# Attention bias in an encoder layer on Trainium2: from flip products on TensorE to a skewed copy in DRAM and additions on VectorE

## What is computed

```python
bias = rel_table[rel_bucket(kpos[None, :] - qpos[:, None])]
bias = jnp.transpose(bias, (2, 0, 1)).astype(jnp.float32)
visible = (kpos[None, :] // CHUNK) <= (qpos[:, None] // CHUNK)
s = jnp.einsum('bqhmd,bkhmd->bhmqk', qblk, k).astype(jnp.float32)
s = s + bias[None, :, None]
s = jnp.where(visible, s, -jnp.inf)
p = jax.nn.softmax(s, axis=-1)
attn = p[:, :, 0] - lam * p[:, :, 1]
```

## Time and profile before

| | |
|---|---|
| median of 3 runs | 537.84 us (536.12 to 542.68) |
| the profiled execution | 541.47 us, of which 539.7 us is the span of the profile |
| PE busy | 511.6 us, 95% of the span |
| DVE busy | 246.5 us, 46% |
| ACT busy | 196.8 us, 36% |
| DMA | 149.29 MB, mean 277 GB/s |
| chain that ended last | issue 46%, PE 40%, DVE 8%, DMA 3% |

### The profile page before, as it was taken

The page is one execution under the profiler, slowest core; times in us unless marked ns, Lnnn a source line. Parts: engine busy times, 40 slices in busy tenths (PEclk is TensorE's granted clock), DMA queues, the critical chain, the costliest instruction groups (busy, mean ns, idle before and its releaser), DMA issues.

```text
span 539.7 us, 7303 instructions
## 1 busy us (share of the span) xinstructions
PE 511.6 (95%) x2868; PEld 345.8 (64%) x2868; DVE 246.5 (46%) x466; ACT 196.8 (36%) x347; POOL 15.6 (3%) x30
## 2 busy tenths in 40 slices
PE   8799999899999999999989988999999999999782
PEld 7798998688888888898978533433443344333231
DVE  4473499967778679975652611111111111111113
ACT  6353567464736355354565202110211021101013
POOL 2000010000040000000000000000000000000000
PEclk9989999999999999999998899999999999999997
DMA  7777547633655548976997599999999999999982
GB/s 245 238 268 205 161 122 233 199 90 117 175 177 164 167 149 249 364 257 184 367 346 264 187 335 389 387 387 386 387 386 386 387 386 387 387 386 388 385 303 82
DMA packets 81835, 149.29 MB, mean 277 GB/s; under 512 B 8262, under 2 KB 11524, under 8 KB 81796
## 3 DMA queue, kind: packets, MB, share of 16 engines
q1 hardware_dynamic: 81780, 148.76, 80.2%
q10 hardware_dynamic: 16, 0.00, 0.0%
HBM read 147.69 MB, written 1.05 MB: 276 GB/s over the span
## 4 chain that ended last, share of the span: by engine, by line
issue 46%; PE 40%; DVE 8%; DMA 3%; ACT 2%; SPq 0%; POOLq 0%; POOL 0%; ACTq 0%; DVEq 0%
PE bank L1349 11%; PE bank L1351 11%; PE bank L1350 11%; DMA raw<-in_w_in 3%; DVE wl L877 3%; PE bank L1372 1%; PE bank L1468 1%; DVE xc L893 1%; ACT wh L539 1%; PE bank L1491 1%; PE bank L1465 1%; DVE big L923 1%; DVE al L863 1%; DVE big L1171 1%; DVE small L1160 0%
## 5 line engine op out<-in xcount | busy, mean ns | idle before, releaser
L877 DVE TENSOR_TENSOR wl<-raw,wh 128x1024 fp32r<-128x1024 f32 (+1 forms) x80 | 94.2, 1195 | 45.9 <-ACT wh L539 44.5
L539 ACT ACTIVATE wh<-raw 128x1024 fp32r<-128x1024 f32 (+1 forms) x80 | 82.2, 1042 | 79.2 <-PE bank L1351 60.5
L1349 PE MATMUL bank<-wh,ah 128*128 128x512 f32 (+2 forms) x248 | 93.8, 378 | 0.0
L1351 PE MATMUL bank<-wh,al 128*128 128x512 f32 (+2 forms) x248 | 92.8, 374 | 0.0
L1350 PE MATMUL bank<-wl,ah 128*128 128x512 f32 (+2 forms) x248 | 92.7, 374 | 0.0
L1276 DVE TENSOR_TENSOR kT<-bank,normg 64x512 f32<-64x512 f32 x16 | 11.0, 688 | 130.3 <-ACT normg L771 130.3
L1349 PE MATMUL bank<-ah,wh 128*128 128x256 f32 x176 | 51.2, 291 | 3.5 <-DVE wl L877 2.9
L1351 PEld LDWEIGHTS bank<-wh,al 128*128 128x128 f32 x248 | 46.7, 188 | 8.6
L1349 PEld LDWEIGHTS bank<-wh,ah 128*128 128x128 f32 x248 | 46.7, 188 | 8.1
L1350 PEld LDWEIGHTS bank<-wl,ah 128*128 128x128 f32 x248 | 46.7, 188 | 7.9
L1351 PE MATMUL bank<-ah,wl 128*128 128x256 f32 x176 | 50.5, 287 | 0.0
(11 more groups left out here) (330 smaller groups left out, 833.7 us busy)
## 6 DMA issues: line engine op xcount, KB each, us to landing
raw<-in_w_in SPq DMA_DIRECT2D x48, 512.0 KB, 4.4
gates<-in_w_exp_gate SPq DMA_DIRECT2D x15, 512.0 KB, 10.7
gates<-in_w_exp_up SPq DMA_DIRECT2D x15, 512.0 KB, 11.4
wh_raw<-in_w_exp_gate SPq DMA_DIRECT2D x15, 512.0 KB, 10.5
wl_raw<-in_w_exp_up SPq DMA_DIRECT2D x15, 512.0 KB, 11.5
raw<-in_w_branch SPq DMA_DIRECT2D x12, 512.0 KB, 3.9
conv_raw<-in_w_exp_up SPq DMA_DIRECT2D x10, 512.0 KB, 11.5
raw<-in_w_exp_gate SPq DMA_DIRECT2D x10, 512.0 KB, 10.8
```

Of the source, the lines that this page charges most:

```text
L539: act.activation(dst, src, ACT.Copy, scale=scale).then_inc(done, 1)
L877: dve.tensor_tensor(wl[:, n % RING, 0:sz], raw[:, n % RING, 0:sz], wh[:, n % RING, 0:sz].bitcast(F32), ALU.subtract)\
L1349: pe.matmul(dst, st[0], mv[0], start=start, stop=False, skip_group_check=True)
L1351: return pe.matmul(dst, st[1], mv[0], start=False, stop=stop, skip_group_check=True)
```

## The change

- `scratch` in DRAM becomes [4, 128, 384]. One DMA writes each head's run 128 times, from the same four partitions of `pr`.
- `toep` becomes [128, 4, 384] and is read with a step of 383 elements between partitions, starting at element 127 of the first copy: each query's row then stands in its own partition, unflipped, 256 columns for block t = 1 and 128 for t = 0. That takes two DMAs for each head instead of one.
- GpSimd masks both blocks, on partitions 0 to 63; it no longer builds `flip`.
- PE makes the four score products of a head alone; the four flip products go.
- VectorE adds the bias while it moves the scores from PSUM to `pr` in SBUF, one addition of 128 x 384 for each m, and takes the maxima from there, two reductions for both m instead of four. ScalarE's exponentials work in place in `pr`.
- The score banks are given back to PE after the additions (`score_biased`) instead of after the exponentials.
- `vec` (parameters that PE transposes early) moves into `pr`, columns 512 to 639.

```diff
-        toep = sb("toep", [P, HEADS, S])
+        toep = sb("toep", [P, HEADS, S + P])
-        vec = sb("vec", [50, P])
+        vec = pr[0:50, 512:512 + P]
-        scratch = nc.dram_tensor("bias_runs", [HEADS, 384], F32, kind="Internal").ap()
+        scratch = nc.dram_tensor("bias_runs", [HEADS, P, 384], F32, kind="Internal").ap()
...
-                    sp.dma_start(scratch, run[:, 0:384]).then_inc(s_("run_out"), 16)
+                    sp.dma_start(scratch, run[:, 0:384].unsqueeze(1).to_broadcast([HEADS, P, 384])).then_inc(s_("run_out"), 16)
...
                     for h in range(HEADS):
-                        sp.dma_start(toep[:, h, :], bass.AP(scratch.tensor, 384 * h, [[1, P], [1, S]]))\
-                            .then_inc(s_("toep_in"), 16)
+                        for at, lo, w in ((0, 0, S), (S, P, P)):
+                            sp.dma_start(toep[:, h, at:at + w], bass.AP(scratch.tensor, 384 * P * h + P - 1 + lo, [[383, P], [1, w]]))\
+                                .then_inc(s_("toep_in"), 16)
...
-            link(g.memset(flip[:, :], 0.0))
-            link(g.affine_select(out=flip[:, :], in_=flip[:, :], compare_op=ALU.not_equal, fill=1.0, base=-(P - 1),
-                                 pattern=[[1, P]], channel_multiplier=1))
...
-            g.wait_ge(s_("toep_in"), 16 * HEADS)
-            g.memset(toep[64:P, :, S - SEEN:S], LOW).then_inc(s_("toep_ready"), 1)
+            g.wait_ge(s_("toep_in"), 16 * 2 * HEADS)
+            for hi in (S, S + P):
+                g.memset(toep[0:64, :, hi - SEEN:hi], LOW).then_inc(s_("toep_ready"), 1)
...
-                for m, src in enumerate((pS1, pS0)):
+                for m in range(2):
                     for j, (lo, hi) in enumerate(((0, 256), (256, 384))):
-                        act.activation(pr[:, 384 * m + lo:384 * m + hi], src[:, lo:hi], ACT.Exp, bias=mx[:, 2 * m + j:2 * m + j + 1],
+                        p_ = pr[:, 384 * m + lo:384 * m + hi]
+                        act.activation(p_, p_, ACT.Exp, bias=mx[:, 2 * m + j:2 * m + j + 1],
...
             def score_max(h):
+                if h == 0:
+                    dve.wait_ge(s_("toep_ready"), 2)
                 dve.wait_ge(s_("scores_pe"), h + 1)
                 for m, src in enumerate((pS1, pS0)):
-                    for j, (lo, hi) in enumerate(((0, 256), (256, 384))):
-                        ins = dve.tensor_reduce(mx[:, 2 * m + j:2 * m + j + 1], src[:, lo:hi], AX.X, ALU.max)
+                    dve.tensor_tensor(pr[:, 384 * m:384 * m + 384], src[:, 0:384], toep[:, h, :], ALU.add).then_inc(s_("score_biased"), 1)
+                dve.wait_ge(s_("score_biased"), 2 * h + 2)
+                for j, (lo, hi) in enumerate(((0, 256), (256, 384))):
+                    ins = dve.tensor_reduce(mx.rearrange("p (m j) -> p m j", j=2)[:, :, j],
+                                            pr[:, :].rearrange("p (m n) -> p m n", m=2)[:, :, lo:hi], AX.X, ALU.max)
...
                 if h:
-                    pe.wait_ge(s_("score_exp"), 4 * h)
+                    pe.wait_ge(s_("score_biased"), 2 * h)
...
-                    pe.matmul(d, qT[QK * m:QK * m + QK, h, P * t:P * t + P], kT[QK * m:QK * m + QK, h, 0:w],
-                              start=(t == 1), stop=False, skip_group_check=True)
-                for t, w, lo, _, d in blocks:
-                    mm = pe.matmul(d, flip[:, :], toep[:, h, lo:lo + w], start=False, stop=True, skip_group_check=True)
+                        mm = pe.matmul(dst[:, 256 * (1 - t):256 * (1 - t) + w], qT[QK * m:QK * m + QK, h, P * t:P * t + P],
+                                       kT[QK * m:QK * m + QK, h, 0:w], start=(t == 1), stop=True, skip_group_check=True)
```

More of the change, by code:

```diff
@@ L175, in program @@
         ident = sb("ident", [P, P])
-        flip = sb("flip", [P, P])
         upper = sb("upper", [P, P])
         ones = sb("ones", [P, P])
-        vec = sb("vec", [50, P])
+        vec = pr[0:50, 512:512 + P]
         vecT = sb("vecT", [P, 50])
@@ L1460, in scores @@
                 if h:
-                    pe.wait_ge(s_("score_exp"), 4 * h)
-                blocks = [(t, w, lo, m, dst[:, 256 * (1 - t):256 * (1 - t) + w])
-                          for t, w, lo in ((1, 256, 0), (0, 128, 128)) for m, dst in enumerate((pS1, pS0))]
-                for t, w, _, m, d in blocks:
-                    pe.matmul(d, qT[QK * m:QK * m + QK, h, P * t:P * t + P], kT[QK * m:QK * m + QK, h, 0:w],
-                              start=(t == 1), stop=False, skip_group_check=True)
-                for t, w, lo, _, d in blocks:
-                    mm = pe.matmul(d, flip[:, :], toep[:, h, lo:lo + w], start=False, stop=True, skip_group_check=True)
+                    pe.wait_ge(s_("score_biased"), 2 * h)
+                for t, w in ((1, 256), (0, 128)):
+                    for m, dst in enumerate((pS1, pS0)):
+                        mm = pe.matmul(dst[:, 256 * (1 - t):256 * (1 - t) + w], qT[QK * m:QK * m + QK, h, P * t:P * t + P],
+                                       kT[QK * m:QK * m + QK, h, 0:w], start=(t == 1), stop=True, skip_group_check=True)
                 mm.then_inc(s_("scores_pe"), 1)
@@ L1530, in _ @@
                             mm.then_inc(s_("pool_pe"), 1)
-                    pe.wait_ge(s_("toep_ready"), 1)
                     for nm in ("q", "k"):
@@ L1543, in _ @@
                 if s == 4:
-                    pe.wait_ge(s_("score_exp"), 4 * HEADS)
+                    pe.wait_ge(s_("score_biased"), 2 * HEADS)
                     pe.wait_ge(s_("silu_done"), 3)
```

## The result

| | before | with the change |
|---|---|---|
| median | 539.1 us (4 runs, 536.12 to 542.68) | 570.76 us (4 runs, 568.53 to 573.02) |
| ratio | 1 | 1.0574, 95% interval 1.0527 to 1.0620 |
| profiled execution, span | 541.47, 539.7 us | 573.02, 571.3 us |

What follows compares the result with a forecast made beforehand. PE's progress before about 310 us was taken to bound the kernel. Stall 24.1, clock 1.7 and attention 2.3 made 28.1 us, giving 569.6 us for the profiled execution and 566 as the median; range 541 to 573.

Steps and rivals of the forecast that it cites:

- What bounds it: Before about 310 us PE's progress sets the weight stream's start, so a microsecond lost there arrives at the end undiminished.
- The write of the runs: Around 28 us: 786 KB in 512 rows from four partitions share one path of 25.4 GB/s, taking 31 us; chance 0.64.
- T: The duration of the write of the runs, taken as 31 us.
- B: Rival on the write: four engines work side by side, 10 us, total 545 us; chance 0.19.
- C: Rival on the write: spread wider or source cached, under 6.9 us and hidden, total 540 us; chance 0.10.
- 4/128 of the full rate: Full-rate loads spread over 128 partitions, so four neighbouring partitions were never seen to pass more than 13 GB/s.
- four completion marks: Four packets under 512 bytes at 29.0 to 30.0 us, read as showing that the small write used four of 16 engines.
- The stall: PE waits for chunk 8, whose load queues behind the write: T - 6.9 us, 24.1 us with T = 31.
- The clock: After PE's long idle time the granted clock falls to 0.72 over 6 us: 1.7 us lost.
- The flip products go, VectorE's chain grows: Attention slots: PE saves 5.4 us, VectorE gains 1.05 us a head, so the stage ends 2.3 us later.
- my replay: Slot-by-slot timing of the four heads, with PE idle 1.7, 2.5, 0.9 and 2.5 us ahead of their transposes.
- At nothing: Four more reads of `toep` (2 us at most if their cover went), masks, earlier bank release and moved `vec` cost nothing.

Runs made afterwards that it cites:

- bias moved behind the scores: The changed kernel with runs built in and written from 128 partitions, plus the gate block's bias addition and tanh moved behind the score work: 544.55 us, ratio 1.0063.
- woven order: The changed kernel with runs written from 128 partitions, other VectorE work between maxima and mixing, ScalarE's copies ahead of the exponentials: 538.96 us, ratio 0.9959.
- the variant at full clock: The changed kernel with the small write of before, `toep` read with a step of 1, bias rows in reversed order: 541.82 us, ratio 1.0013.
- the wide variant: The changed kernel, but VectorE builds the runs in all 128 partitions and the write reads each partition's own copy: 543.71 us, ratio 1.0046.

## Why the prediction was right, and where it was off

**What bounds it.** Right. A loss on PE before 310 us arrives at the end: the added time is 33.4 us at the logits' products and 31.6 at the end, and the 1.9 between them is the stretch of 13 or 15 us, which I take for chance.

**The write of the runs.** The step that decides. T was taken as 31 us and came out as 32.5, since the path carried 24.2 GB/s where I had put one engine's 25.4; rivals B (10 us) and C (under 6.9) are each seen in a variant with another source (8.5 us, 3.1 us), so they were true of other writes and not of this one. The argument of 4/128 of the full rate was loose (only an absence of evidence), and the variants put it on firm ground. The "four completion marks" were read rightly (the large write has four as well), but they say only how many engines, not how many paths.

**The stall.** 24.1 us forecast, 26.7 measured. The formula chunk 8 = 29.5 + T + 1.3 + 2.3 was off in two terms: the first packet came at 31.1 and not 29.5, 1.4 us behind an issue that itself started 1 us later and took 0.78 us instead of 0.28, and T was 1.5 us longer. The term of 1.3 us held: the last completion mark of chunk 8 (64.89 us) comes 1.28 us behind that of the write (63.61), and ScalarE starts 0.35 us later. With 0.3 us there and 0.2 in copy and subtraction, that is 3.6 us late, less the 1.0 by which PE itself came later. That the issue of chunk 8's load would take 9.3 us, and that nothing of the loads would flow until 40 us, was not foreseen; it did no harm, because the parts on the write's four engines come last anyway.

**The clock.** 1.7 us forecast, 2.5 measured at chunk 8, because PE ran at the low level past 72 us here, where the row I took it from the earlier trace rows averages 0.72 over 6 us. A second fall at slot 0, 1.0 us, was not foreseen. It is no plain sequel of the stall: it is there in the changed kernel and in the variants with partitions 0 to 3 and 0, 4, 8, 12, but also in two variants with no stall (bias moved behind the scores; woven order), and not in the two with idle products. PE waits 1.9 us ahead of slot 0 in every trace, and the clock falls behind it in some. What decides that is open.

**The flip products go, VectorE's chain grows.** 2.3 us forecast for the stage, 2.2 measured, 2.2 in the variant at full clock. Per head 1.05 us forecast and 1.06 measured, but that close by luck, as two errors cancel: additions and reductions take 2.05 us and not 2.20 (no wait of 0.15 for its own additions shows), and the wait for ScalarE's exponentials, now in place from SBUF, is 1.93 us and not 1.78, which I had counted as the same. Where PE waits was half wrong: I had all of it ahead of the transposes (1.7, 2.5, 0.9, 2.5); at full clock it is 1.45 there for head 0, then 1.27 + 0.66, 0.08 + 0.28, and 1.76 + 0.28, of which the first parts stand ahead of `attn_o`. They add up to 5.8 us and not to the 7.6 of my replay, and the stage is as long all the same, because, by the same estimate, a wait costs more than the idle time shown. ScalarE's copies for `attn_o` lie behind the exponentials in its order, so the same lateness of VectorE reaches PE first by that way.

**At nothing.** The eight reads of `toep` and the masks: between chunk 8 and slot 0 the trace shows no loss beside the clock's (2.5 us against 2.6 by the clock's levels), and none at all in the wide variant (63.5 us), which reads `toep` in the same eight transfers.

**The sum.** 28.1 forecast, 31.6 measured on the profiled executions. Of the difference of 3.5, 2.7 is the stall, 0.8 + 1.0 the clock, 1.0 the late start, -0.1 the stage and -1.9 the stretch before the experts. The two that I take for chance, 1.0 and -1.9, come to -0.9, towards the forecast. The rest up to 570.76 is that before had a median of 539.1 over four runs, 1.3 above the one I set out from.

## What to carry to other kernels

Before a broadcast in DRAM is built from a few rows in SBUF, count the groups of four partitions that the source touches, not the bytes and not the engines: 786 KB took 31 to 32.5 us out of one group, 8 to 8.5 out of four and 3.1 out of all. Price a DMA by the loads that stand behind it in its queue. When work is moved off an engine, compare its start times with the end of the chain it waits for: where these are a few tenths apart, as in the earlier trace rows, the saving is spent on waiting until the other engine's order of work is changed too.

## What the runs showed that I had not expected

- One slow DMA holds the queue: the issue of the next four loads took 21.4 us behind it, 3.4 us behind the wide one. The first of them alone took 9.3 us, and until 40 us no data of the loads moved, though 12 engines had nothing to do with the write.
- The clock's cost hardly depends on how long PE stood idle. Chunk 8 to slot 0 took 66.1 to 66.2 us after 26.7, 25.4 and 4.07 us of idle time, and 63.5 to 64.0 after 1.16 or none. The stall of 4.07 us thus cost 4.1 + 2.7 + 0.8 = 7.6 us up to the first scores, with the second fall at slot 0. (One trace; the time of that execution was 5.4 us over its kernel before.)
- The clock also fell about waits of 0.7 to 3 us in the slots: in the changed kernel at 155 us, in the wide variant at 125 us, and at 132 to 139 us, around a wait of 2.98 us, in the variant with the bias moved behind the scores.
- A packet of 1,536 bytes took 68 ns with a path to itself and 210 to 232 ns with four engines on that path. A DMA share of 90% in the profile (partitions 0 to 15) stood beside 102 GB/s: busy engines are not a sign of a full rate.
- ScalarE's exponentials in place in SBUF were 0.15 us a head slower than out of PSUM.
